# Twenty convolution products in the chunk inversion, output steps ahead of memory transposes, and reordered mixers

## What is computed

```python
z = h @ w_in                      # u, q, f, i, g: 512 columns each
pooled = moving_mean(u, windows 2, 4, 8, 16 for the four groups) - u
a_out = (pooled @ pool_w) * pool_scale        # 4 products of 128 channels
logf, k = log_decay(f), (1 - lb) * sigmoid(-f)
o = hgrn2_chunkwise(q, k, i, logf)            # 4 heads of 128, decayed scores and a state
b_out = rmsnorm(o) * silu(g)
y = concatenate([a_out, b_out]) @ w_out
```

## Time and profile before

| | us |
|---|---|
| three runs | 3412.44, 3419.03, 3421.88 |
| median | 3419.03 |
| the profiled execution | 3421.45 |
| its span | 3420.1 |

### The profile page before, as it was taken

One profiled execution on the slowest core, in us unless ns is written; L12 is line 12 of the kernel. 1 busy time (PEld: TensorE's weight loads), 2 busy tenths in 40 slices (PEclk: granted clock), 3 DMA queues, 4 the chain that ended last, 5 costly groups with the idle time before them and its releaser, 6 DMA issues.

```text
span 3420.1 us, 48064 instructions
## 1 busy us (share of the span) xinstructions
PE 3229.4 (94%) x18545; PEld 2729.7 (80%) x18545; DVE 2234.2 (65%) x3834; ACT 1358.5 (40%) x2195; POOL 1625.0 (48%) x897
## 2 busy tenths in 40 slices
PE   8987999999999999999897998999999998999997
PEld 8876778888776778888576646899999998888886
DVE  5576656555445656542586646168998995888888
ACT  5544444223444443222443224333333774333332
POOL 1342324444332324443332012458888445888885
PEclk9998999999999999999998999999999999999999
DMA  8410214444321314432220011349899899999995
GB/s 258 151 65 30 95 50 136 140 132 148 97 88 44 105 50 136 148 131 91 71 74 8 15 62 62 124 155 333 305 323 318 267 311 309 378 351 353 351 365 210
DMA packets 304819, 584.76 MB, mean 171 GB/s; under 512 B 13521, under 2 KB 224465, under 8 KB 287313
## 3 DMA queue, kind: packets, MB, share of 16 engines
q1 hardware_dynamic: 252512, 373.32, 32.3%
q0 software_dynamic: 42576, 153.83, 12.6%
q10 hardware_dynamic: 9504, 54.53, 4.2%
HBM read 522.91 MB, written 58.72 MB: 170 GB/s over the span
## 4 chain that ended last, share of the span: by engine, by line
PE 76%; DVE 11%; issue 4%; POOL 4%; ACT 4%; DMA 1%; POOLq 0%; DVEq 0%; SPq 0%; ACTq 0%
PE bank L487 18%; PE bank L489 18%; PE bank L488 18%; PE twin L487 3%; PE twin L489 3%; PE twin L488 3%; PE bank L2910 2%; POOL split_low L464 2%; PE bank L2335 2%; PE bank L568 1%; PE bank L2142 1%; DVE residual L682 1%; DMA rows_arena<-in_peer_v_rows,own_expert 1%; ACT normed_high L597 1%; DVE rows_near L3077 1%
## 5 line engine op out<-in xcount | busy, mean ns | idle before, releaser
L464 POOL TENSOR_TENSOR split_low<-weights,split_high 128x1024 fp32r<-128x1024 f32 x520 | 1270.6, 2449 | 1421.6 <-ACT split_high L456 1411.4
L487 PE MATMUL bank<-normed_high,split_high 128*128 128x384 f32 (+1 forms) x2016 | 742.9, 368 | 24.7 <-ACT normed_high L597 14.0
L489 PE MATMUL bank<-normed_high,split_low 128*128 128x384 f32 (+1 forms) x2016 | 732.5, 363 | 0.0
L488 PE MATMUL bank<-normed_low,split_high 128*128 128x384 f32 (+1 forms) x2016 | 732.4, 363 | 0.0
L456 ACT CAST split_high<-weights 128x1024 fp32r<-128x1024 f32 x554 | 571.3, 1046 | 348.5 <-PE bank L489 198.6
L487 PEld LDWEIGHTS bank<-normed_high,split_high 128*128 128x128 f32 x2016 | 381.5, 189 | 73.9 <-ACT normed_high L597 16.4
L488 PEld LDWEIGHTS bank<-normed_low,split_high 128*128 128x128 f32 x2016 | 381.5, 189 | 40.7 <-issue 2.2
L489 PEld LDWEIGHTS bank<-normed_high,split_low 128*128 128x128 f32 x2016 | 380.8, 189 | 40.5
L487 PE MATMUL bank<-split_high,wide_hidden_high 128*128 128x512 f32 x768 | 300.8, 392 | 10.8 <-DVE wide_hidden_low L3132 5.8
L488 PE MATMUL bank<-split_low,wide_hidden_high 128*128 128x512 f32 x768 | 300.2, 391 | 0.0
L489 PE MATMUL bank<-split_high,wide_hidden_low 128*128 128x512 f32 x768 | 300.0, 391 | 0.0
(11 more groups left out here) (636 smaller groups left out, 6267.5 us busy)
## 6 DMA issues: line engine op xcount, KB each, us to landing
weights<-in_w_ff SPq DMA_DIRECT2D x64, 1024.0 KB, 5.5
weights<-in_peer_u SPq DMA_DIRECT2D x64, 1024.0 KB, 6.8
weights<-in_peer_v SPq DMA_DIRECT2D x64, 1024.0 KB, 8.9
weights<-in_cond_w SPq DMA_DIRECT2D x24, 1024.0 KB, 5.4
early_table<-branch SPq DMA_DIRECT2D x128, 192.0 KB, 4.3
gate_table<-arena SPq DMA_DIRECT2D x12, 2048.0 KB, 10.2
lates<-early_table ACTq DMA_DIRECT2D x32, 768.0 KB, 9.6
gates<-gate_table ACTq DMA_DIRECT2D x32, 768.0 KB, 12.4
```

The costliest lines, as they stand in the source:

```text
L464: pool.do.tensor_tensor(lo, raw_unit(u), hi.bitcast(F32), ALU.subtract).then_inc(*pool.sig("split_low", u))
L487: pe.do.matmul(o, ah, bh, start=first, stop=False)
L488: pe.do.matmul(o, ah, bl, start=False, stop=False)
L489: return pe.do.matmul(o, al, bh, start=False, stop=last)
```

## The change

- **Even mixer.** The weight stream is reordered. One q unit stays ahead of the loop; the other three and u go into it in halves of a unit (`pe_product_steps`), so 22 turns hold a piece where 12 did. Poolings stand at turns 13, 15, 22 and 29, for groups 2, 3, 0, 1. Two output steps stand in turns 33 and 35; `pe_first` takes its channel tiles in another order. The gating multiplications move into the loop. The low halves of 22 units, 12 of them in the loop, go from POOL to DVE, one turn behind ACT's cast.
- **Memory mixers.** Two output steps stand in slot 11, ahead of its transposes; slots 12 and 13 have none.
- **RW stage.** POOL waits for the last residual sum ahead of its first splits; `rw_masks` is loaded from ACT's queue. Twenty taps go into the inversion; 10 are left after the scan. ACT reads the first tile's bank in the scan. DVE centres the convolution ahead of the low halves.

The diff, cut to its core (eight columns of indentation removed). Not shown: the pooled matmul moves behind the pairs and one turn later, ACT's copy of it too; the wait for the h tiles before they are overwritten is for the last u unit; `dve_pooling` follows `U_ORDER`.

```diff
-W["E", "i"] = []
-for n, first, n_cols in (("f", 0, 512), ("g", 0, 512), ("q", 0, 512), ("i", 0, 256), ("u", 0, 512), ("i", 256, 256)):
-    ids = stream(dram["w_in_ab"], n0="uqfig".index(n) * 512 + first, n_cols=n_cols)
-    W["E", n] = W["E", "i"] + ids if n == "i" else ids
+for n in "qiu":
+    W["E", n] = []
+for n, first, n_cols in (("f", 0, 512), ("g", 0, 512), ("q", 0, 256), ("i", 0, 256), ("u", 256, 256),
+                         ("q", 256, 256), ("u", 0, 256), ("i", 256, 256)):
+    W["E", n] = W.get(("E", n), []) + stream(dram["w_in_ab"], n0="uqfig".index(n) * 512 + first, n_cols=n_cols)
-EARLY = 2 * W["E", "f"][0] + 2
+def pe_product_steps(stage, ids, rhs, ready, emptied):
+    for c in range(2 * len(ids)):
+        ck = chunks[ids[c // 2]]
+        u, cols = weights(ck, c % 2)
+        bank, empty = banks.take("product", stage, c)
+        pe.wait_ge(empty, split_ready(u))
+        for a in range(CT):
+            pe.wait_ge(ready(a))
+            last = triple(bank, [w_[:, a, cols] for w_ in unit_tiles(u)], rhs(a), a == 0, a == CT - 1)
+            if a == CT // 2 - 1:
+                yield
+        last.then_inc(*pe.sig("product", stage, c))
+        banks.give(("product", stage, c), *emptied(c))
+        used[u] = ("product", stage, c)
+        yield
...
 N_TURNS = len(REC_ITEMS) + 4
-I_TURNS, U_TURNS = (4, 6, 8, 10, 19, 21, 23, 25), (11, 13, 15, 17)
-PIECE_TURNS = sorted(I_TURNS + U_TURNS)
-UNIT_PIECE = (3, 3, 4, 5, 6, 7, 11, 11)
-HEAD_FINALS, POOL_FINALS = {27: 0, 28: 1, 35: 2}, {29: 0, 30: 1, 31: 2, 32: 3}
+REC_PIECES = {4: "q", 5: "q", 6: "i", 7: "i", 8: "i", 9: "i", 10: "u", 11: "u", 12: "u", 13: "u", 14: "q", 15: "q",
+          16: "q", 17: "q", 19: "u", 20: "u", 22: "i", 23: "i", 24: "i", 25: "i", 27: "u", 28: "u"}
+I_TURNS = [n for n in REC_PIECES if REC_PIECES[n] == "i"]
+Q_ENDS, U_ENDS = [{n: j // 2 for j, n in enumerate(m for m in REC_PIECES if REC_PIECES[m] == kind) if j % 2} for kind in "qu"]
+U_ORDER = (2, 3, 0, 1)
+UNIT_FREE = (4, 5, 9, 9, 11, 13, 15, 17, 20, 28, 29, 30)
+GATED = {0: 0, 5: 1, 6: 2, 7: 3}
+POOLING = {13: 2, 15: 3, 22: 0, 29: 1}
+HEAD_FINALS, POOL_FINALS = {29: 0, 30: 1, 35: 2}, {31: 2, 32: 3, 33: 0, 34: 1}
+FIRST_TURNS = (33, 35)
+FIRST_ORDER = (4, 5, 2, 3, 0, 1, 6, 7)
 def pool_at(n, delay):
-    g = (n - 14 - delay) // 2
-    return [g] if (n - delay) % 2 == 0 and 0 <= g < 4 else []
+    return [POOLING[n - delay]] if n - delay in POOLING else []
 def rec_units(n):
-    return 2 * W["E", "i"][0] + 3 - (n < 5) + sum(PIECE_TURNS[j] < n for j in UNIT_PIECE)
+    return 2 * W["E", "q"][0] + 3 + sum(free < n for free in UNIT_FREE)
+def h_read():
...
-    run(pe_product((EM, "q"), W["E", "q"], h_tile, ready, scaled_out((EM, "q"))))
-    i_product = pe_token_product((EM, "i"), W["E", "i"], h_tile, ready, lambda n, tk: [("rec_v", n, tk)], TT)
-    u_product = pe_product((EM, "u"), W["E", "u"], h_tile, ready, scaled_out((EM, "u")))
+    pieces = {"q": pe_product_steps((EM, "q"), W["E", "q"], h_tile, ready, scaled_out((EM, "q")))}
+    for _ in range(2):
+        next(pieces["q"])
+    pieces["i"] = pe_token_product((EM, "i"), W["E", "i"], h_tile, ready, lambda n, tk: [("rec_v", n, tk)], TT)
+    pieces["u"] = pe_product_steps((EM, "u"), W["E", "u"], h_tile, ready, scaled_out((EM, "u")))
+    first = pe_first((EM, "o"), W["E", "o"], h_tile, mixed(EM), y_copied(EM), T, FIRST_ORDER)
     for n in range(4, N_TURNS):
...
             outputs = pe_rec_output(hd - 1) if hd else iter(())
-        if n in PIECE_TURNS:
-            next(i_product if n in I_TURNS else u_product)
-        for g in pool_at(n, 1):
...
         bank, empty = banks.take("pairs", hd, lv)
         left, right = (e_k[:, hd, :], e_q[:, hd, :]) if lv == 0 else [factor.tile("factor", hd, lv)] * 2
...
+        if n in FIRST_TURNS:
+            next(first)
     outputs = pe_rec_output(REC_HEADS - 1)
-    first = pe_first((EM, "o"), W["E", "o"], h_tile, mixed(EM), y_copied(EM))
-    for _ in range(TT):
+    for _ in range(TT + 1):
         next(outputs)
         next(first)
-    next(outputs)
-    next(first)
-    next(first)
...
     for c in range(4):
         act_split(2 * W["E", "g"][0] + c + AHEAD)
-        for _ in range(4):
-            next(decays)
+        for _ in range(8):
+            next(decays, None)
...
+    act_split(2 * W["E", "q"][0] + AHEAD)
...
     for c in range(4):
+        dve_split(2 * W["E", "f"][0] + c + AHEAD)
...
-    for c in range(5):
-        if c < 4:
-            dve_scaled((EM, "g"), [c], lambda c: e_gate[:, c, :])
-        if c:
-            dve_decay(c - 1)
-    for c in range(4):
-        dve_scaled((EM, "q"), [c], lambda c: e_q[:, c, :])
-        dve.wait_ge(at("gate_sigmoid", c))
-        dve.do.tensor_tensor(e_gate[:, c, :], act_tmp.tile("gate_sigmoid", c), e_gate[:, c, :], ALU.mult
-                             ).then_inc(*dve.sig("gated", c))
+    dve_scaled((EM, "g"), [0], lambda c: e_gate[:, c, :])
+    dve_split(2 * W["E", "g"][0] + AHEAD)
+    dve_decay(0)
+    for c in range(1, 4):
+        dve_decay(c)
+        dve_scaled((EM, "g"), [c], lambda c: e_gate[:, c, :])
+        dve_split(2 * W["E", "g"][0] + c + AHEAD)
...
+        if n in GATED:
+            c = GATED[n]
+            dve.wait_ge(at("gate_sigmoid", c))
+            dve.do.tensor_tensor(e_gate[:, c, :], act_tmp.tile("gate_sigmoid", c), e_gate[:, c, :], ALU.mult
+                                 ).then_inc(*dve.sig("gated", c))
+        elif n == 3:
+            dve_scaled((EM, "q"), [0], lambda c: e_q[:, c, :])
+            dve_split(2 * W["E", "q"][0] + AHEAD)
...
-        if n in U_TURNS:
-            dve_scaled((EM, "u"), [U_TURNS.index(n)], lambda c: upad[:, c, POOL_PAD:])
+        if n > 4:
+            dve_split(rec_units(n - 1))
+        if n in Q_ENDS:
+            dve_scaled((EM, "q"), [Q_ENDS[n] + 1], lambda c: e_q[:, c, :])
+        if n in U_ENDS:
+            dve_scaled((EM, "u"), [U_ENDS[n]], lambda c: upad[:, U_ORDER[c], POOL_PAD:])
         for g in pool_at(n, 0):
             dve_pooling(g)
...
 def pool_even():
     pool.do.dma_start(rec_masks, dram["rec_masks"]).then_inc(*pool.land("rec_masks_landed"))
     pool.do.dma_start(keep_tile, dram["keep_tile"]).then_inc(*pool.land("keep_tile_landed"))
-    pool_split(2 * W["E", "q"][0] + 3 + AHEAD - 1)
     pool.wait_ge(at("decay_step", 3))
...
     for n, (hd, lv) in enumerate(REC_ITEMS):
-        pool_split(rec_units(n))
         if lv:
...
-    pieces.update((m, ("o",)) for m in (12, 13, 15, 16, 19, 20))
+    pieces.update((m, ("o", n)) for m, n in ((11, 2), (15, 1), (16, 1), (19, 1), (20, 1)))
...
     for c in range(4):
         pe_gram(("gram_n", c), b_hat[:, c, :], a_hat[:, c, :], None, lambda hh: ("n_kept", c, hh))
         if c:
+            conv_some(taps, 3 if c == 1 else 0)
             pe_turns(("x_turned", 0, c - 1), Y[:, c - 1, :], at("inv_start", c - 1), inv_kept("x", 0, c - 1))
+    conv_some(taps, 2)
     pe_turns(("x_turned", 0, 3), Y[:, 3, :], at("inv_start", 3), inv_kept("x", 0, 3))
...
             if c:
+                conv_some(taps, 3 if c == 4 else 0)
                 pe_turns(("y_turned", lv, c - 1), X[:, c - 1, :], at("inv_x", lv, c - 1), inv_kept("y", lv, c - 1))
...
     act_rw_products()
+    act.wait_ge(at("product", (RM, "ab"), 7))
+    act.do.dma_start(rw_masks, dram["rw_masks"]).then_inc(*act.land("rw_masks_landed"))
     meet(act, "act", "rw_prepared")
...
         act.wait_ge(at("scan_old", ch))
...
+        if ch == 2:
+            act_conv(CONV_PE[0])
     meet(act, "act", "rw_scanned")
-    act_conv(CONV_PE[0])
     act_split(2 * W["R", "o"][0] + 1)
...
         act_tmp.give(("square", f"gn{c}", 0), ("summed", f"gn{c}", 0))
+    act_conv(CONV_PE[1])
     for c in range(4):
         act_root(f"gn{c}", 0, GN_EPS, n_[c])
-    act_conv(CONV_PE[1])
     act_split(2 * W["R", "o"][0] + AHEAD)
...
         dve.do.tensor_tensor(yc, yc, banks.tile("lora_g", c), ALU.mult).then_inc(*dve.sig("rw_gated", c))
+    dve_conv_end(0)
     for c in range(4):
         dve.wait_ge(at("mixed_high", RM, 4 + c))
...
-    for step in (0, 3, 4):
+    for step in (3, 4):
         dve_conv_end(step)
...
     conv_some(taps, 2)
 def pool_rw():
+    pool.wait_ge(at("x_dve", "mlp1", CT - 1))
     pool_split(2 * W["R", "p"][0] + AHEAD)
-    pool.wait_ge(at("product", ("mlp1", "down", FF_GROUPS - 1), CT - 1))
     pool.do.dma_start(lora, dram["lora"]).then_inc(*pool.land("lora_landed"))
     pool.do.dma_start(g2, dram["rw_g2"]).then_inc(*pool.land("g2_landed"))
     pool.do.dma_start(keep_chunk, dram["keep_chunk"]).then_inc(*pool.land("keep_chunk_landed"))
     pool_split(last_unit(("R", "ab")))
-    pool.wait_ge(at("product", (RM, "ab"), 7))
-    pool.do.dma_start(rw_masks, dram["rw_masks"]).then_inc(*pool.land("rw_masks_landed"))
     meet(pool, "pool", "rw_prepared")
```

More of the change, by code:

```diff
@@ L1380, in pe_mem @@
                     pe_token_root(st, root, TT, 0)
-                elif piece == ("o",):
-                    next(first_o)
```

(3 more changed lines are left out.)

24 lines of the change are left out of this document (14 added, 10 removed).

## The result

The changed kernel takes 3364.57 us in the median of four runs (3356.46 to 3368.29), the kernel before 3417.57 (four runs, 3412.44 to 3421.88): a ratio of 0.9842, with a 95% interval of 0.9819 to 0.9865, so 53 us less. The forecast was 3371 in 3350 to 3398. The profiled execution of the changed kernel is the fastest of the four: 3356.46 us, span 3355.1. One execution of the kernel before, among those beside e5 to e8, took 17390.85 us and is left out of the ratios.

The account below looks back on a forecast made before the run. TensorE, busy 94% of the span, bounds the kernel; gains only from its holes, low clock or moved serial-end work. Terms -20 - 2 - 8 - 3 + 2 - 17 = -48 from 3421.45 give 3373.5, median 3371 us, range 3350 to 3398.

Parts of the forecast that it names:

- Even mixer, -20: Even mixer's loop and tail: q units and steps fill PE's holes, 20 us less, ends -32 and -5.
- The relief of the port, put at 16 us: Even mixer's loop: DVE's two-input operations get 16 us shorter once POOL's splits no longer run beside them.
- Rival C: Even mixer's loop: the port lock turns round, DVE's twelve splits hold POOL's factor, +14.6 us, 3386; chance 0.08.
- Memory mixers, -2: Both memory mixers: two output steps ahead of slot 11's transposes take PE's bank wait, 1 us less each.
- Residual add, -8: End of mlp1: POOL's splits wait for the last residual sum, so DVE's adds finish 8.2 us earlier; 8 us less.
- Masks, -3: Meeting: masks issued from ACT's queue remove POOL's 6.2 us drain, about 3 us left to gain, ends 0 and -4.5.
- Inversion, +2: Inversion: twenty taps, 18.6 us, against 15.0 us of holes, less some clock gain; 2 us longer, ends +20 and -4.
- rival B: Inversion: the taps run at the low clock, 1.85 us each, 19.6 us more, 3391; chance 0.10.
- Behind the scan, -17: After the scan: 10 taps instead of 30, and centring directly behind the group-norm chain; 17 us less, ends -12 and -21.5.
- rival A: Even mixer: DVE paces the loop, no port stalls come back, gain 5 instead of 20 us, 3386; chance 0.15.
- D: Even mixer's loop: DVE stands at each of twelve splits until ACT has cast, serial turns, 3451 us; chance 0.03.
- E: Whole kernel: the change doesn't do what it says, A, B and C together, 3420 us, no difference; chance 0.04.

Follow-up runs that it names:

- e5: The changed kernel with the twelve low halves of the even mixer's loop back on POOL, one turn earlier: 3364.46 us, ratio 0.9844 to the kernel before.
- e8: The kernel before with the even mixer's 22 low halves on DVE, nothing reordered: 3415.91 us, ratio 0.9996.
- e9: The changed kernel with all four q units, their weights and scaling ahead of the even mixer's loop: 3380.70 us, ratio 0.9897 to the kernel before.
- e6: The changed kernel without output steps in turns 33 and 35, all eight behind the loop: 3356.80 us, ratio 0.9827 to the kernel before.
- e11: The changed kernel without output steps in the loop and with the output weights' four casts directly after the scan: 3350.85 us, ratio 0.9806 to the kernel before.
- e4: The changed kernel with memory mixers' output steps, POOL's missing wait and masks on POOL's queue as before: 3378.60 us, ratio 0.9883 to the kernel before.
- e2: The kernel before with twenty further 128x512 matmuls, results overwritten, at the taps' places in the inversion: 3414.17 us, ratio 0.9993.
- e1: The changed kernel with the twenty taps and ACT's two convolution bank reads back in their old places: 3384.74 us, ratio 0.9898 to the kernel before.
- e10: The changed kernel with ACT's casts of the output weights' third and fourth units directly behind the first two: 3355.30 us, ratio 0.9828 to the kernel before.
- e12: The changed kernel measured and profiled again, nothing altered: 3365.39 us, ratio 0.9843 to the kernel before.

## Why the prediction was right, and where it was not

The whole, -48 forecast and -53 measured in the medians, is right in its likeliest case. The three large terms hit. That the sum comes so close is in part luck: in the last column of the table inversion and meeting gave 13.2 us more than forecast, and 8.7 of that is taken back by the even mixer, the memory mixers, the RW products behind the add, and the scan.

- **Even mixer, -20:** -17.3 to -20.0 in seven profiles. The cause is the one named, work for PE's holes: e9 without q gives nothing, e8 and e5 put the port at 2 to 3 us. The forecast took 20 of 43.5 us of slack; left are 19.1 us of holes and 0.05 x 115.0 = 5.8 us of low clock in the loop. The relief of the port, put at 16 us, was about right: from the first decay difference to the last mask DVE is busy for 107.9 us instead of 101.8, though 13 splits (16.2 us), four scalings and three gate products (4.8) are added, so the operations that both kernels have take some 15 us less. Rival C was real in its mechanism, 5.4 us on POOL's factor, and without effect on the time: POOL was idle for 90 us of the loop, and the profile shows no wait of PE there that ends on it. What failed inside is the two output steps that "come forward" as a gain: without them the even mixer is some 2.5 us shorter (e6, e11), because the tail needed them.
- **Memory mixers, -2:** nothing (e4). "The wait mostly moves" was all of it: PE waits 2.4 us at the first output step for the same low half, where it waited 3.0 at the transposes.
- **Residual add, -8:** -8.2. "PE waits for nothing else" hid a cost: the RW products took 2.4 to 2.6 us more in every kernel with the wait and no more in e2 and e4. Not the splits, which are hidden as forecast: PE's first product starts 13.8 us behind the last sum in both kernels. It is the clock: this part is granted 0.97 where it was 0.99, and 0.99 again in e4:

```profile
1615.40:1769.00 153.60, 144.22 (x584) 108.98 (x584) 102.20 (x112) 76.69 (x107) 57.74 (x25) 0.97 0.26 82
```

  Two hundredths of 144 us busy are 2.9 us. In the kernel before, 13.7 us at 0.50 lie in the add, where PE has 6.2 us of work; in the changed kernel 6.8 us at 0.50 lie in the add and 6.8 at the start of the products:

```profile
1630.10:1643.80 13.70, 6.23 (x7) 2.25 (x8) 13.53 (x11) 0.75 (x1) 10.56 (x7) 0.50 0.50 152
1627.40:1634.20 6.80, 5.51 (x13) 4.38 (x14) 6.60 (x11) 3.88 (x6) 0.00 (x0) 0.50 0.57 202
```

  Why the low clock falls there is open; in e8, which has no such wait, these products took 1.6 us more as well.
- **Masks, -3:** 3.1 for the drain, as forecast. The terms missing, 3.2 us, lie in the grams: DVE's wait for PE's first gram, 1.0 us, and the low clock behind the drain, about 2 (e4).
- **Inversion, +2:** -9.7 us, the largest error. Twenty taps, 18.6 us, against 15.0 us of holes made +3.6, and that was right as far as it went: PE's idle time fell by 11.5 us, and its busy time, the clock aside, rose by 14.4 (from 77.3 to 91.7). The step that failed is the next, "a PE that stands still less may be granted 2.4 rather than 1.2 GHz for more of it (0.86 now), so I take +2": it credited 1.6 us to a clock that cost 0.14 x 89.9 = 12.6 us, and rival B had it turned round. 14.4 - 11.5 - 12.6 are the -9.7. The taps were never at 1.85 us; they took away all or nearly all of the low clock. That the clock follows the work put into the stage is shown by e1, e2 and e4: the three profiles without taps or filling there have 0.86, 0.87 and 0.89 (before, e1, e8), all the others 0.98 to 1.00. What decides where the low clock falls is not shown.
- **Behind the scan, -17:** -17.1, with its parts: two splits held DVE for 3.4 us (4 forecast), and e10 takes these back: -20.5, near the forecast's end of -21.5., from which the prediction concludes that an operation reading PSUM doesn't stretch, hold none that does; L1271 shows it, 732 ns in the loop beside POOL's splits and 734 without them now, and so do the 0.69 us between the two splits. And not only operations with two inputs stretch, as e5's copy shows.

Against rival A stands e5, where DVE has 7.9 us more work and the loop takes 3.1 more. Rivals D and E are excluded by e8 and the whole. One slip in the range: the inversion at -4 is 6 us below +2, not part of the "three more" that lead to 3350, so the low end should have been some 3 us or more lower.

## What to carry to other kernels

In a stage of small dependent matmuls, reckon what its low clock costs as well as its holes: (1 - granted clock) times the busy time, 12.6 us here, is what filling could win beyond them. Independent matmuls from a dense stage are worth most there; here the stage got shorter even by useless ones (e2), though the whole of e2 did not move clear of its interval. Before a step is moved forward into a loop, see whether the tail behind it has anything else to do.

## What the runs showed of the hardware

Twenty 128x512 matmuls added to a stretch of 108.5 us made it 9.7 us shorter (e2). PE's granted clock in the scan, 0.90 or 1.00, a difference of 6.2 us, was not the same for the same code: 1.00 in the changed kernel's first profile and 0.90 in e12, 0.90 in e1 to e4, 1.00 in e5 to e11, and 0.95 in the kernel before. A POOL multiplication of 128x256 took 897 ns where POOL makes the splits (1002 in e5) and 1091 where DVE makes them. A DVE copy of 128x8 took 2.20 us beside a POOL split, and 171 ns without (e5).
